# One decoder step on one core: where in TensorE's order the second sum of squares of a norm stands, and which sample windows a mixer product waits for

## The reference, cut to what matters

```python
def rms_norm(x, g):
    y = xf * lax.rsqrt(jnp.mean(xf * xf, axis=-1, keepdims=True) + EPS)
...
op, st_p = pool_mix(hp, pool_zero, 0, pool_w[j], pool_scale[j])   # windows 2, 4, 8, 16 on 4 channel groups
os_, st_s = pool_mix(hs, state_pool[j], past, pool_w[j], pool_scale[j])
xp = xp + g_mp[:, None, :] * rms_norm(op, norm_mix_post[i])
hp = modulate(xp, norm_ffn_pre[i], sh_fp, sc_fp)
fp, cst_p = conv_ffn(hp, conv_zero, ffn_w_up[i], ffn_conv_w[i], ffn_conv_b[i], ffn_w_down[i])
xp = xp + g_fp[:, None, :] * rms_norm(fp, norm_ffn_post[i])
```

## Time and profile before

| what | us |
|---|---|
| median of 3 runs | 2554.91 |
| lowest and highest run | 2552.56, 2557.10 |
| the profiled execution, its own time | 2561.38 |
| the span of its instructions | 2558.7 |
| mean granted clock of TensorE | 0.98 |

### The profile page before, as it was taken

One profiled execution on the slowest core, in us unless ns is written; L12 is line 12 of the kernel. 1 busy time (PEld: TensorE's weight loads), 2 busy tenths in 40 slices (PEclk: granted clock), 3 DMA queues, 4 the chain that ended last, 5 costly groups with the idle time before them and its releaser, 6 DMA issues.

```text
span 2558.7 us, 40501 instructions
## 1 busy us (share of the span) xinstructions
PE 2416.8 (94%) x15148; PEld 2067.1 (81%) x15148; DVE 1671.3 (65%) x2953; ACT 1216.9 (48%) x2726; POOL 332.4 (13%) x365
## 2 busy tenths in 40 slices
PE   7989999998988899999999999999989999999996
PEld 5966666765668777888999999987777789999996
DVE  5656666665234578666687767758855787766666
ACT  4444444443234545443556455545544455444443
POOL 0000000000004240000131022024122202100003
PEclk9989999999999999999999999999999999999998
DMA  7022223226532222232322222233222222232221
GB/s 271 13 92 91 98 105 115 105 101 226 192 142 92 66 83 92 98 99 95 102 76 75 75 75 91 76 107 104 74 79 79 81 92 83 83 116 83 83 83 68
DMA packets 71714, 253.50 MB, mean 99 GB/s; under 512 B 7874, under 2 KB 15426, under 8 KB 64610
## 3 DMA queue, kind: packets, MB, share of 16 engines
q1 hardware_dynamic: 71090, 250.78, 28.5%
q10 hardware_dynamic: 432, 0.15, 0.0%
HBM read 243.83 MB, written 7.07 MB: 98 GB/s over the span
## 4 chain that ended last, share of the span: by engine, by line
PE 53%; DVE 10%; ACT 3%; issue 3%; POOL 2%; DMA 0%; DVEq 0%; ACTq 0%; POOLq 0%
PE psum L2743 11%; PE psum L2742 11%; PE psum L2744 11%; PE psum L2706 6%; PE psum L2707 6%; PE psum L2708 6%; DVE t_conv L2530 3%; DVE t_w_lo L2511 3%; POOL t_stat L2102 1%; PE psum L2178 1%; DVE t_y L2563 1%; ACT t_w_hi L2380 1%; PE psum L2684 1%; PE psum L2685 1%; PE psum L2686 1%
## 5 line engine op out<-in xcount | busy, mean ns | idle before, releaser
L2742 PE MATMUL psum<-t_h,t_w_hi 128*128 128x288 f32 (+1 forms) x2112 | 700.3, 332 | 0.0
L2743 PE MATMUL psum<-t_h,t_w_hi 128*128 128x288 f32 (+1 forms) x2112 | 695.6, 329 | 0.0
L2744 PE MATMUL psum<-t_h,t_w_lo 128*128 128x288 f32 (+1 forms) x2112 | 694.2, 329 | 0.0
L2742 PEld LDWEIGHTS psum<-t_h,t_w_hi 128*128 128x128 f32 x2112 | 399.2, 189 | 32.4
L2743 PEld LDWEIGHTS psum<-t_h,t_w_hi 128*128 128x128 f32 x2112 | 398.9, 189 | 32.2
L2744 PEld LDWEIGHTS psum<-t_h,t_w_lo 128*128 128x128 f32 x2112 | 399.2, 189 | 28.4
L2563 DVE TENSOR_TENSOR t_y<-psum,t_y 128x288 f32<-128x288 f32 (+1 forms) x480 | 254.8, 531 | 238.7 <-PE psum L2708 237.2
L2380 ACT ACTIVATE t_w_hi<-t_raw 128x1024 fp32r<-128x1024 f32 x280 | 294.5, 1066 | 244.4 <-PE psum L2708 234.7
L2511 DVE TENSOR_TENSOR t_w_lo<-t_raw,t_w_hi 128x1024 fp32r<-128x1024 f32 x280 | 342.6, 1236 | 94.2 <-ACT t_w_hi L2380 93.8
L2530 DVE SCALAR_TENSOR_TENSOR t_conv<-t_u,t_taps,t_conv 128x512 f32<-128x512 f32 (+2 forms) x440 | 310.3, 705 | 125.7 <-ACT t_conv L2418 120.5
L2706 PE MATMUL psum<-t_g_hi,t_w_hi 128*128 128x288 f32 (+1 forms) x1056 | 349.8, 331 | 20.1 <-DVE t_y L2563 10.6
(11 more groups left out here) (215 smaller groups left out, 3364.8 us busy)
## 6 DMA issues: line engine op xcount, KB each, us to landing
t_raw<-in_ffn_w SPq DMA_DIRECT2D x264, 512.0 KB, 3.5
late_w<-in_ada_late SPq DMA_DIRECT2D x40, 1024.0 KB, 4.8
cache<-in_cache SPq DMA_DIRECT2D x64, 320.0 KB, 4.7
t_raw<-in_wo SPq DMA_DIRECT2D x16, 512.0 KB, 3.3
ada_w<-in_ada_w SPq DMA_DIRECT2D x6, 1024.0 KB, 9.7
proj_raw<-in_proj_w SPq DMA_DIRECT2D x8, 448.0 KB, 9.0
x<-in_pair_w SPq DMA_DIRECT2D x4, 768.0 KB, 5.3
x<-in_x SPq DMA_DIRECT2D x1, 2304.0 KB, 11.7
```

The source lines that it names most:

```text
L2742: pe.matmul(bank, t.w_hi[s][:, o], hi, start=kt == 0, stop=False)
L2743: pe.matmul(bank, t.w_hi[s][:, o], lo, start=False, stop=False)
L2744: last = pe.matmul(bank, t.w_lo[s][:, o], hi, start=False, stop=kt == KT - 1)
```

## The change

In the plans of half 1 the second tick of each pair of sums is moved: in `BETWEEN[1]` from 15, 39, 81 and 105 to 17, 41, 83 and 107, in `AFTER_OUT_B` from 9 and 33 to 12 and 35. There the first step on the samples goes from tick 12 to 14. `BETWEEN[0]` keeps its numbers. In `Chain.pe` a mixer product of half 1, piece 1, waits for the sample windows of its own group and those before it, not for all four.

```diff
 AFTER_OUT_B = Plan(
-    [("y", IN_ORDER, [two_each(1), two_each(5)], (9, 9), paced(11), (12, 18, 24)),
-     ("x", IN_ORDER, [[t + 2 for t in paced(11)[0]], [25, 25] + list(range(26, 32))], (33, 33), None, None)],
+    [("y", IN_ORDER, [two_each(1), two_each(5)], (9, 12), paced(11), (14, 18, 24)),
+     ("x", IN_ORDER, [[t + 2 for t in paced(11)[0]], [25, 25] + list(range(26, 32))], (33, 35), None, None)],
...
-    [("y", IN_ORDER, Y_SQUARES[half], (15, 15), paced(17), (18, 24, 30)),
+    [("y", IN_ORDER, Y_SQUARES[half], (15, 15 + 2 * half), paced(17), (18, 24, 30)),
...
             if self.half and lc:
-                pe.wait_ge(t.window_f, self.after["window_f"])
+                pe.wait_ge(t.window_f, self.at["window_f"] + len(POOL_BY_POOL) + g + 1)
```

## The result

| | median us | runs | lowest to highest |
|---|---|---|---|
| before | 2556.01 | 4 | 2552.56 to 2560.81 |
| changed | 2534.56 | 4 | 2531.93 to 2536.27 |

The ratio is 0.9914, with a 95% interval of 0.9895 to 0.9933: 21.5 us faster, 17 to 27 by the interval. The forecast was 2526.5 with 2534 as its upper end, so the direction was right and the size was not. The profiled execution of the changed kernel took 2534.93 us (span 2533.0), that of before 2561.38 (2558.7). The difference of these two is 26.5, five more than that of the medians; the experiments are mostly about that.

The account below looks back on a forecast made before the run. PE was taken as the bound, held up by POOL's late adds. 22.85 - 0.4 + 3.2 + 2.8 = 28.45 us gained: 2532.9 off the profiled execution, 2526.5 off the median; range 2521 to 2534.

Parts of the forecast that it names:

- Part 1: Five sums moved four positions on: PE's waits for POOL's adds and the low clock go, gaining 22.85 us.
- Part 3: Sum moved from tick 9 to 12, first quarter: POOL wait becomes 4.1 us for `t_w_lo`; gain 3.2, bounds 2.9 and 5.8.
- Part 4: Mixer's second product: wait for DVE becomes 2.1 us for ACT's evacuation; gain 2.8 us, bounds 2.0 and 3.6.
- (a): All named waits go, the sixth sum's and the mixer's too: gain 38.7 us, time 2516.2; 4%.
- (d): The loop of ACT and DVE, not PE, sets the time around the norms; roots add 13.1 us, 2568.0; 3%.
- (e): Squares and POOL's adds come later as the sums move; waits stay, only the mixer's goes, 2552; 3%.
- Rival (c): ACT's table load also drains: extra roots about 1.4 us longer at six places, about 4 lost, time 2530.5; 4%.
- rival (b): DVE partly becomes the bound: late down-product sums give back 1 to 2.5 us per pair, 5 to 13 in all; 12%.
- Part 2: Moved sums' extra roots on ACT, 2.18 us each, at five places ahead of `t_g_hi`: 0.4 us lost, bounds 0 and 0.6.

Follow-up runs that it names:

- half-distance kernel: Kernel before with only five of the six sums moved, each by one tick, from position 8 to 10 instead of 12: 2545.71 us, ratio 0.9950.
- single-load kernel: Changed kernel without the second load of ACT's Ln and Exp table where no SiLU stands between a pair of roots: 2531.56 us.
- the kernel with the later squares: Changed kernel with the last four squares of the sixth norm piece two ticks later, its sum at tick 15, samples' step at 17: 2533.34 us.
- the sixth sum alone: Kernel before with only the sum moved from tick 9 to 12 and the samples' step from 12 to 14: 2553.43 us, ratio 0.9984.
- the mixer's wait alone: Kernel before with only the mixer product's wait cut to its own sample group: 2553.82 us, ratio 0.9984.
- the five sums alone: Kernel before with only the five sums that move four positions within their pair; mixer's wait and remaining sum as before: 2540.39 us, ratio 0.9936.

## Why the prediction missed its size

**Where it was right.** The mechanism held at all six places and at the mixer product. Part 1, the five sums, came to 22.72 us in the trace against 22.85 summed. Part 3's new wait was 4.03 against 4.1, with a low clock behind it. Part 4's wait that is left was 2.17 against 2.1. The half-distance kernel shows why: POOL's end stands still, so a wait shrinks by exactly the PE work put before it. Rivals (a), (d) and (e) did not happen. Rival (c), the drain of the table load, is refuted: in the changed kernel each of the 19 loads from `L1856` is 1.28 us, and Ln follows within 0.02 us in 18 of them (1792.33 + 1.28, then 1793.63); at the last ACT waits 1.51 us for PE's sum, as in the kernel before. Of rival (b) there are traces only, new or longer waits for DVE, each below 0.7 us, where it had 1 to 2.5 in each of five pairs.

**Small terms that were mis-sized.** Part 2 had 0.4 us for pair 7 and what hangs on it. `t_g_hi` was late by 0.62 as said (0.58), but pair 7 lost 0.53 and pair 8 another 0.92, less 0.32 in pair 9: 1.1 us. Pair 7's loss goes with the late `t_g_hi` and DVE's work behind it. Pair 8's is clock: PE's wait of 1.90 us stands there in the kernel before too, but in the five profiles with the extra load in pair 7 the clock fell behind it, and in the nine without it it did not. Pair 6 of the first quarter and pair 18 of the third, put at 0, lost 0.18 each. Part 3's gain was 2.75, not 3.2. The prediction priced five extra roots and left out that of the sixth sum: its load costs 1.4 us in pairs 2 and 3, as the single-load kernel shows. Part 4 gave 3.4, not 2.8, since the low clock stayed away. That was luck in part: behind the same wait it came in the kernel with the later squares. In all the stage gained 27.3 us where the sum said 28.45.

**The step that failed** is the last line of the sum: "off the median of 2554.91 the same sum gives 2526.5". About 9 of the 22.85 us, 3 of the sixth sum's old loss and 2 of the mixer's were low clock behind a wait, and they were priced from one execution. That execution stood 6.5 us above the median, which the prediction itself states and does not use. Taken off that execution the sum gave 2532.9, and the changed kernel's profiled execution took 2534.93; it is the step to the median that broke. (That median, 2554.91, was itself 1.1 us under the 2556.01 of the four runs.) The runs showed what the 6.5 us meant: after the same wait of 2.77 us the clock fell in two profiles (23.38 and 23.37 us) and did not in two others (20.58 twice).

Two ways give the size. By the slope of 0.36 over the 38 runs the first profiled execution paid 4.6 us more for low clock than the typical one, which a change that takes waits away can't save in the typical run; 27.3 less 4.6 is 22.7. The second way needs no slope. Give the stage of the sixth sum alone back its own 2.8 us, and that of the mixer's wait alone its 3.3, and the stage of before comes to 1659.9 and 1660.4, against 1664.87 in the first profile. Against these the changed kernel gains 22.3 to 22.8 and the five sums alone 15.3 to 15.8; measured were 21.5 and 16.4. The bounds of parts 3 and 4 allowed for the clock; part 1, with most of it, had no bound at all for it. The waits of part 1 alone are 13.0 us and 0.16 at each place, 13.8; with these the lower bound of the gain would have been 13.8 - 0.6 + 2.9 + 2.0 = 18.1 us, and the range would have held the time.

What is not settled: the second measurement of the change gave 27 us, with an interval that holds the forecast gain of 28.45, and the kernel before was 5 us slower in that session. Whether its runs met more low clock at the waits by chance or by that chip, or ahead of the stage, can't be told from these runs: a timed run gives one mean clock for the whole program. That the first profiled execution was dear inside the stage and not ahead of it is seen in its trace: its stage began at 854.53, within the 851.96 to 857.94 of all 14 profiles.

## What to carry to other kernels

A wait in an in-order queue that ends at a time which the queue itself does not set can be had back in full, up to the work that is put ahead of it; look at once for what the next instruction needs, since that takes over where the margin was smaller. Count what the moved work drags along on the other engines too, here a table load with each root. Split the cost of a stall in two, the wait itself and the low clock behind it: the first repeats to the hundredth of a us from run to run, the second may be there or not, and its size in one profile is not a mean. A change to another engine, upstream, can bring a low clock behind a wait that itself stays as it was. Compare the clock of the profiled execution with that of the timed runs before a sum is taken off their median.

## What the runs showed of the hardware

The granted clock after the same wait in the same code fell in some executions and not in others. In the four profiles in which the old places are untouched (the kernel before twice, the sixth sum alone, the mixer's wait alone) it fell after the wait of 2.77 us in two of four. After 2.26 us it fell at the place in pair 6 of the third quarter in all four, at that in pair 17 in two, and after 2.27 in pair 5 of the first quarter in none. After 1.90 us in pair 8 of the third quarter it fell in the five profiles with an extra table load in pair 7 and in none of the other nine. In the half-distance kernel it did not fall after 0.88 us at three places nor after 1.38 at one. So the length of the wait alone does not say it, and what does is not shown here. By the difference of the same pair with and without it, a fall cost 0.9 us (pair 8), 1.6 (pair 17) and 2.8 (pair 13).

A load of ACT's table costs its 1.28 us also where the set is in place already, with no load of another set since: the moved root took 2.18 us with it (1792.33 to 1794.51) and 0.89 without (1788.44 to 1789.33).
